# The first layer of a filter network: from VectorE, woven between weight splits, to a program of its own on GpSimd

## The chip, the cores and the metric

One core of a Trainium2 chip runs the whole program once. The metric is the device time of that run in microseconds (us). A kernel's time is the median of its runs. Engines are named as the profile names them: PE is the matrix engine (TensorE), DVE the vector engine (VectorE), ACT the scalar engine (ScalarE), POOL the GpSimd engine, SP the sync engine, which here only issues transfers. "SPq", "DVEq" and "ACTq" are those engines' sequencers.

## What is computed

The reference is two transformer-like blocks over 256 tokens of width 2048, all in float32. Almost all the time goes into products of token rows with large weight matrices. In the second block a convolution filter is made from positions by a small network, and its first layer is what the change moves:

```python
z = jnp.concatenate([t[:, None], jnp.cos(ang), -jnp.sin(ang)], axis=-1)   # 256 positions x 33
fr = freq.astype(f32)
h = jnp.sin(fr * (z @ w1 + b1))      # 33 -> 64: the first layer
h = jnp.sin(fr * (h @ w2 + b2))      # 64 -> 64
h = jnp.sin(fr * (h @ w3 + b3))      # 64 -> 64
h = h @ w4                           # 64 -> 2048 taps
```

`freq` and the inputs are scaled up so far (by 64) that the sum in front of the first sine must be more exact than float32. The kernel therefore adds the 33 products one by one with compensation: each product is split into parts whose rounding errors are kept, and each addition's error is worked out and added back.

## The kernel before, in words

**The stream of matrix products.** All large products run in one scheme (class Gemm, lines 83 to 107). A product is a row of groups of 512 output columns; with 2048 inputs a group is four chunks of 1 MB of weights. SP brings each chunk into one of four ring slots (`stream`, L357), issuing chunk k as soon as PE is done with chunk k-4. A chunk is used in two parts. For each part ACT makes the high half of the weights (`high`, L370, ring of four), DVE makes the low half by a subtraction (`low`, L379), and PE multiplies (`multiply_group`, L401): 12 matmuls a part of 128x512, 96 a group. ACT may write part p's high half only when PE is through with part p-4. So each engine works some parts ahead of PE, and the whole is one chain SP, ACT, DVE, PE.

**The stretch in question.** After the first block's input product comes `g_o` (4 groups, the first block's output weights), then, after a normalisation for which PE has to wait, `g_i2` (17 groups, numbered 0 to 16 here, the second block's input weights, 2048 to 8704 columns). Behind it comes the filter and the convolution.

**Work woven in.** DVE's side work is a generator, `filter_and_heads`, that `Spare` steps after each part's `low`, with a share of 1.4 us a part by costs that are written beside each `yield`. A generator may also yield a part number, before which it isn't stepped on. In the kernel before it clears `h3T` (the accumulator, 128 x 128: 64 hidden units of two halves of the positions), runs 11 steps `filter_sum(e)` of 3 inputs each, then `hidden_layer(0)` (bias, frequency and sine), then, at parts (12, 3) and (13, 3) of `g_i2`, `hidden_layer(1)` and `hidden_layer(2)`. For each input `filter_sum` issues 13 operations on 128x128 tiles (L1460, L1462, L1464) in 8 stages, with a semaphore wait at the end of each stage. Four of the 13 are the fused form, product and addition in one (L1464).

**Inputs of the sums.** `embedding(e)` (L2118 on, transfers at L2130) has SP bring the 3 inputs of step e, two transfers of 128 x 9 rows of values, into one of two slots of `z_k`. Step e of 2 and later waits first for `z_used` to be e-1, that is for step e-2 to be done with its slot. SP is one queue: while it waits there no weights are issued. The places in the stream are fixed by `EMBED_AFTER`: steps 0 and 1 behind the loads of group 0 of `g_o`, step 2 behind group 2, step 3 behind group 3, and steps 4 to 10 behind groups 1, 2, 3, 4, 6, 7 and 8 of `g_i2`. The last chunk of a group is issued when PE is done with the last chunk of the group before, so SP comes to a group's embedding just when PE starts that same group.

**The later layers.** PE computes the second and third layers as matmuls behind groups 11 and 12 of `g_i2` (L482 by way of `mm`), after waits for `sin1` and `sin2`, which DVE's sines signal.

Of the kernel before, what the change touches and what calls it, by code (L numbers as in the profile page):

```python
# [9 lines left out]
F32 = mybir.dt.float32  # L10
# [5 lines left out]
P = 128  # L16
# [25 lines left out]
EMB, HID = 33, 64  # L42
FK = 3
# [36 lines left out]
AT_AT = 124  # L80
MIX_AT = 146
LEAD = 3
LAYER_AFTER = (11, 12)
EMBED_AFTER = (0, 0, 2, 3, 5, 6, 7, 8, 10, 11, 12)
QK2_ROOT_GROUP = 15

# [51 lines left out]
def build(nc, a, out):  # L138
    Gemm.chunks = Gemm.groups_before = 0
    ctx = ExitStack()  # L140
    with ctx:
# [3 lines left out]
        def sb(name, shape, dt=F32, stack=ctx):  # L145
            return stack.enter_context(nc.sbuf_tensor(name, shape, dt))

        st = ExitStack()
# [3 lines left out]
        st = ExitStack()  # L152
# [25 lines left out]
        h3T = sb("h3T", [P, P])  # L178
        w1T = sb("w1T", [P, 3, 36])
# [3 lines left out]
        st = ExitStack()  # L183
# [3 lines left out]
        st = ExitStack()  # L187
# [2 lines left out]
        at_buf = sb("at_buf", [P, 4, P], F32, st)  # L190
        state = sb("state", [P, 2, 3, P], F32, st)
        dec = sb("dec", [P, NH, 4], F32, st)
        zero_t = sb("zero_t", [P, P], F32, st)
        st.close()
        st = ExitStack()
        sb("index_below", [P, HRING * HT * GW], F32, st)
# [6 lines left out]
        st = ExitStack()  # L203
# [3 lines left out]
        st = ExitStack()  # L207
        sb("filter_below", [P, HRING * HT * GW], F32, st)
        z_k = sb("z_k", [P, 2, 3, FK, P], F32, st)
        f_tmp = sb("f_tmp", [P, 6, P], F32, st)  # L210
        st.close()
        st = ExitStack()
        sc_s = sb("sc_s", [P, 4, SEQ], F32, st)
# [3 lines left out]
        st = ExitStack()  # L217
# [7 lines left out]
        st = ExitStack()  # L225
# [3 lines left out]
        st = ExitStack()  # L229
# [3 lines left out]
        st = ExitStack()  # L233
# [3 lines left out]
        st = ExitStack()  # L237
# [5 lines left out]
        st = ExitStack()  # L243
# [6 lines left out]
        st = ExitStack()  # L250
# [4 lines left out]
        st = ExitStack()  # L255
# [5 lines left out]
        st = ExitStack()  # L261
# [20 lines left out]
        st = ExitStack()  # L282
        hbuf = sb("hbuf", [P, TT, D], F32, st)
        st.close()
        st = ExitStack()
# [5 lines left out]
        st = ExitStack()  # L291
# [25 lines left out]
        g_i2 = Gemm([(w2v, 0)], KT, 17)  # L317
# [122 lines left out]
        def sig(name):  # L440
            if name not in signals:
                signals[name] = sem(name)
            return signals[name]

        block = ctx.enter_context(nc.Block())
# [34 lines left out]
        def _(pe):  # L480
# [117 lines left out]
            def recurrence():  # L598

                yield D_AT[0] - 1  # L600
                pe.wait_ge(sig("lf_ready"), TT)
                pe.wait_ge(sig("masks_in"), 48)
                b = bank(pe, "dec", "a")
                for h in range(NH):
                    for t in range(TT):
                        m = mm(b[:, 4 * h + 2 * t:4 * h + 2 * t + 2], lf[:, t, h * HD:h * HD + HD], ind[:])
                m.then_inc(filled, 1)
                for q, (n, t) in enumerate(((0, 0), (0, 1), (1, 0), (1, 1))):
                    if q == 3:
                        yield from turn_scaled(0)  # L610
                    for j in range(3):
                        yield D_AT[q] + j
                        mm(bank(pe, ("D", t, n, j), "a")[:, :], tri[:, j], lf[:, t, n * GW:n * GW + GW]).then_inc(filled, 1)
                yield from turn_scaled(1)
                pe.wait_ge(sig("zero_ready"), 1)
                for h in range(NH + 1):
                    if h < NH:
                        yield HEAD_AT + 2 * h
                        inside(h)
                    if h >= 1:  # L620
                        yield HEAD_AT + 2 * h + 1
                        recur(h - 1)
# [133 lines left out]

            for j in range(g_i2.groups):
                multiply_group(pe, g_i2, j, halves, turn_h2 if j == 0 else None)
                if j in LAYER_AFTER:
                    n = LAYER_AFTER.index(j)  # L760
                    pe.wait_ge(sig(f"sin{n + 1}"), 1)
                    mm(bank(pe, ("layer", n), "v")[:, 0:P], w23[:, n], h3T[:]).then_inc(filled, 1)

# [100 lines left out]
        def _(dve):  # L864
# [3 lines left out]
            def link(ins):  # L868

                links[0] += 1  # L870
                ins.then_inc(v_chain, 1)
                dve.wait_ge(v_chain, links[0])
# [215 lines left out]
            link(v.tensor_tensor(wl_, wh_, w_, ALU.subtract))  # L1088
            link(v.tensor_tensor(wh_, wh_, wl_, ALU.subtract))
            link(v.tensor_tensor(wl_, w_, wh_, ALU.subtract))  # L1090

            def before_products():

# [86 lines left out]
            def recurrence():  # L1180
# [9 lines left out]
                for t in range(TT):  # L1190
                    link(v.tensor_scalar(kc[:, t], kc[:, t], -1.0, 1.0, ALU.mult, ALU.add))
                link(v.memset(at_buf[:], 0.0))
                v.memset(zero_t[:], 0.0).then_inc(sig("zero_ready"), 1)
                for m, (n, t) in enumerate(((0, 0), (0, 1), (1, 0), (1, 1))):
                    yield D_AT[m] + 2 * LEAD
                    dve.wait_ge(sig("decays"), 4 * (m + 1))
# [241 lines left out]
                        v.tensor_tensor(x, pair[:], x, ALU.add).then_inc(evac[pair_of(gm, j)], 1)  # L1438
                return step

            def filter_sum(e):

                dve.wait_ge(sig("z_in"), 32 * (e + 1))
                p_, e_, s_, b_, d_, t_ = (f_tmp[:, q] for q in range(6))
                acc = h3T[:]
                for j in range(FK):
                    z_, zh, zl = (z_k[:, e % 2, q, j] for q in range(3))
                    w_, wh, wl = (w1T[:, q, e * FK + j:e * FK + j + 1] for q in range(3))
                    n = 13 * (FK * e + j)
                    for stage in (((p_, z_, w_, None),),  # L1450
                                  ((e_, zh, wh, p_), (s_, acc, p_, ALU.add)),
                                  ((e_, zl, wh, e_), (b_, s_, acc, ALU.subtract)),
                                  ((e_, zh, wl, e_), (d_, s_, b_, ALU.subtract), (t_, p_, b_, ALU.subtract)),
                                  ((e_, zl, wl, e_), (d_, acc, d_, ALU.subtract)),
                                  ((t_, t_, d_, ALU.add),),
                                  ((t_, t_, e_, ALU.add),),
                                  ((acc, s_, t_, ALU.add),)):
                        for o, x, y, last in stage:
                            if last is None:
                                i = v.tensor_scalar(o, x, y, None, ALU.mult)  # L1460
                            elif isinstance(last, ALU):
                                i = v.tensor_tensor(o, x, y, last)  # L1462
                            else:
                                i = v.scalar_tensor_tensor(o, x, y, last, ALU.mult, ALU.subtract if last is p_ else ALU.add)  # L1464
                            i.then_inc(sig("sum_step"), 1)
                            n += 1
                        dve.wait_ge(sig("sum_step"), n)
                        yield 0.33 * len(stage)
                dve.sem_inc(sig("z_used"), 1)

            def hidden_layer(n):

                if n:
# [13 lines left out]
            q2, k2 = heads(proj2, B_Q, NH), heads(proj2, B_K, 2)  # L1487

            def filter_and_heads():
                dve.wait_ge(sig("f_cols_in"), 16 * 8)  # L1490
                link(v.memset(h3T[:], 0.0))
                for e in range(EMB // FK):
                    yield from filter_sum(e)
                yield g_i2.part(1, 2)
                yield from hidden_layer(0)
                for n in range(1, 3):
                    yield g_i2.part(LAYER_AFTER[n - 1] + 1, 3)
                    yield from hidden_layer(n)
                yield g_i2.part(B_G // GW, 4)
                for j in range(B_Q // GW, B_G // GW):  # L1500
                    evacuated(dve, g_i2, j)
                yield from head_squares(q2, NH, HD, hs[:, :, 0:NH])
                yield from head_squares(k2, 2, HD, hs[:, :, NH:NH + 2])
                m = hs[:, :, 0:NH + 2]
                v.tensor_scalar(m, m, 1.0 / HD, EPS, ALU.mult, ALU.add).then_inc(sig("qk2_ms"), 1)
                yield g_i2.part(QK2_ROOT_GROUP, 4)
                dve.wait_ge(sig("ax_in"), 48)
                dve.wait_ge(sig("qk2_root"), 1)
                link(v.reciprocal(hs[:, :, 0:NH + 2], hs[:, :, 0:NH + 2]))
                yield from norm_and_rotate(q2, hs[:, :, 0:NH], gains2[:, 0], ax[:, 0], ax[:, 1], NH, HD, 2)  # L1510
                yield from norm_and_rotate(k2, hs[:, :, NH:NH + 2], gains2[:, 1], ax[:, 0], ax[:, 1], 2, HD, 2)
                dve.sem_inc(sig("qk2_roped"), 2)
# [591 lines left out]
        def _(sp):  # L2104
# [17 lines left out]
            def embedding(e):  # L2122

                if e == 0:
                    sp.wait_ge(sig("mix_a"), 2)
                if e >= 2:
                    sp.wait_ge(sig("z_used"), e - 1)
                for half in range(TT):
                    z = a["z"][half][:, FK * e:FK * e + FK]
                    sp.dma_start(z_k[half * HID:half * HID + HID, e % 2], z.partition_broadcast(HID)).then_inc(sig("z_in"), 16)  # L2130

            def beside_o(j):
                for e in range(EMB // FK):
# [19 lines left out]
            for j in range(g_d.groups):  # L2153
                o = slice(GW * j, GW * j + GW)
                evacuated(sp, g_d, j)
                sp.dma_start(out_rows[:, :, o], x_res[:, :, o]).then_inc(sig("out_written"), 16)
            sp.wait_ge(sig("out_written"), 16 * g_d.groups)


# [94 lines left out]
```

## Time and profile before

| What | us |
|---|---|
| median of 3 runs (2249.16 to 2251.08) | 2249.46 |
| the profiled execution's own time | 2251.36 |
| span of the profiled execution | 2249.6 |
| PE busy in it | 2091.2 (93%) |
| DVE busy | 1430.6 (64%) |
| ACT busy | 902.9 (40%) |
| POOL busy, 4 instructions | 0.2 |

The span is the time from the first to the last instruction in the trace. Times of rows are microseconds from its start; durations of single instructions are in ns where the row says min/median/max or mean ns. "idle before <-X" or "[.. <-X]" tells what ended the idle time of an engine in front of an instruction. A matmul row of PE overlaps the next one, so 96 matmuls of 389 ns take 21.8 us, not 37.

### The profile page before, as it was taken

How to read it: one execution, taken by the hardware profiler on the slowest of the kernel's cores; microseconds unless marked ns; L12 is line 12 of the kernel's file. 1: busy time of each engine (PE TensorE's matmuls, PEld its weight loads, DVE VectorE, ACT ScalarE, POOL GpSimd, SP SyncE). 2: the span in 40 equal slices, each digit the busy share in tenths (PEclk: the TensorE clock that was granted, in tenths of full speed). 3: DMA queues.
4: the chain of work that ended last, by engine and by line, in shares of the span. 5: the costliest groups of instructions: out<-in, count | busy, mean ns of one | idle time of the engine just before them, and what ended most of it. 6: DMA issues, size and time to landing. Idle time of an engine off the chain costs nothing.

```text
span 2249.6 us, 23590 instructions
## 1 busy us (share of the span) xinstructions
PE 2091.2 (93%) x9229; PEld 1644.1 (73%) x9229; DVE 1430.6 (64%) x2224; ACT 902.9 (40%) x1157; POOL 0.2 (0%) x4
## 2 busy tenths in 40 slices
PE   4889999999999798999977788989999999999999
PEld 0258787777878687887853567868888888878887
DVE  4857668677669787886877666555545454444443
ACT  2034523555644433444411343434444444443333
POOL 0000000000000000000000000000000000000000
PEclk8989979999999899999978999989999999999999
DMA  7867656544466475766630035545555555556554
GB/s 283 306 220 270 209 177 210 169 150 150 153 223 207 132 210 198 231 198 201 199 133 0 1 130 169 169 131 188 187 190 193 193 187 190 188 173 200 188 193 163
DMA packets 208498, 408.47 MB, mean 182 GB/s; under 512 B 10826, under 2 KB 16386, under 8 KB 207746
## 3 DMA queue, kind: packets, MB, share of 16 engines
q1 hardware_dynamic: 195056, 382.56, 51.7%
q10 hardware_dynamic: 13330, 24.40, 3.2%
q8 instruction: 73, 1.20, 0.2%
q14 instruction: 39, 0.31, 0.0%
HBM read 404.83 MB, written 2.10 MB: 181 GB/s over the span
## 4 chain that ended last, share of the span: by engine, by line
PE 82%; DVE 11%; DMA 3%; issue 1%; ACT 1%; ACTq 1%; SPq 0%; DVEq 0%
PE ps L401 74%; PE pm L482 5%; DVE raw_lo L379 3%; DMA raw<-in_w_in 2%; DVE mod_part L1144 1%; DMA raw<-in_ada_w 1%; PE ps L482 1%; PE pm L595 0%; DVE f_tmp L1462 0%; PE pm L494 0%; DMA proj<-in_hgrn_lb_logits 0%; PE pm L844 0%; DVE xtmp L1577 0%; ACT w_hi L370 0%; ACTq L1813 0%
## 5 line engine op out<-in xcount | busy, mean ns | idle before, releaser
L379 DVE TENSOR_TENSOR raw_lo<-raw,w_hi 128x1024 fp32r<-128x1024 f32 (+1 forms) x648 | 784.2, 1214 | 597.0 <-ACT w_hi L370 587.6
L370 ACT ACTIVATE w_hi<-raw 128x1024 fp32r<-128x1024 f32 (+1 forms) x648 | 678.2, 1050 | 892.1 <-PE ps L401 842.4
L401 PE MATMUL ps<-w_hi,h_hi 128*128 128x512 f32 (+1 forms) x2336 | 931.9, 399 | 42.1 <-DVE raw_lo L379 24.1
L401 PE MATMUL ps<-w_hi,h_lo 128*128 128x512 f32 (+1 forms) x2336 | 915.1, 392 | 0.0
L401 PE MATMUL ps<-raw_lo,h_hi 128*128 128x512 f32 (+1 forms) x2336 | 914.6, 392 | 0.0
L401 PEld LDWEIGHTS ps<-w_hi,h_hi 128*128 128x128 f32 x2336 | 444.9, 190 | 144.2 <-issue 31.8
L401 PEld LDWEIGHTS ps<-w_hi,h_lo 128*128 128x128 f32 x2336 | 444.8, 190 | 92.8
L401 PEld LDWEIGHTS ps<-raw_lo,h_hi 128*128 128x128 f32 x2336 | 445.3, 191 | 91.3 <-issue 3.8
L401 PE MATMUL ps<-w_hi,hid_hi 128*128 128x512 f32 x256 | 99.9, 390 | 1.8 <-DVE raw_lo L379 1.8
L401 PE MATMUL ps<-raw_lo,hid_hi 128*128 128x512 f32 x256 | 99.6, 389 | 0.0
L401 PE MATMUL ps<-w_hi,hid_lo 128*128 128x512 f32 x256 | 99.6, 389 | 0.0
L482 PE MATMUL ps<-raw,c_sig 128*1 128x512 f32 x128 | 67.2, 681 | 5.8 <-DMA raw<-in_ada_w 5.8
L401 PEld LDWEIGHTS ps<-w_hi,hid_hi 128*128 128x128 f32 x256 | 48.1, 188 | 12.0 <-DVE raw_lo L379 2.1
L401 PEld LDWEIGHTS ps<-w_hi,hid_lo 128*128 128x128 f32 x256 | 48.1, 188 | 10.1
L401 PEld LDWEIGHTS ps<-raw_lo,hid_hi 128*128 128x128 f32 x256 | 48.1, 188 | 9.7
L482 PEld LDWEIGHTS ps<-raw,c_sig 128*1 128x1 f32 x128 | 11.3, 92 | 59.2 <-issue 49.5
L1708 ACT ACTIVATE h_hi<-xtmp 128x256 fp32r<-128x256 f32 x88 | 32.8, 411 | 42.7 <-DVE xtmp L938 25.3
L1170 DVE SCALAR_TENSOR_TENSOR gate<-proj,c_sig,gate 128x512 f32<-128x512 f32 x64 | 48.0, 750 | 1.9
L1464 DVE SCALAR_TENSOR_TENSOR f_tmp<-z_k,w1T,f_tmp 128x128 f32<-128x128 f32 x132 | 46.1, 349 | 2.6
L1144 DVE SCALAR_TENSOR_TENSOR mod_part<-raw,c_sig,mod_part 128x512 f32<-128x512 f32 x56 | 42.1, 752 | 7.8 <-DMA raw<-in_ada_w 6.0
L1829 ACT ACTIVATE mod_row<-ps 1x512 f32<-1x512 f32 x8 | 4.7, 587 | 93.1 <-PE ps L482 93.1
L482 PE MATMUL ps<-mod_part,ones 128*1 128x512 f32 x16 | 9.0, 646 | 30.1 <-DVE mod_part L1144 30.1
(301 smaller groups left out, 1208.6 us busy)
## 6 DMA issues: line engine op xcount, KB each, us to landing
raw<-in_w_in SPq DMA_DIRECT2D x140, 1024.0 KB, 5.3
raw<-in_w_ffn_gate SPq DMA_DIRECT2D x44, 1024.0 KB, 5.2
raw<-in_w_ffn_up SPq DMA_DIRECT2D x44, 1024.0 KB, 5.2
raw<-in_w_ffn_down SPq DMA_DIRECT2D x44, 1024.0 KB, 5.1
raw<-in_ada_w SPq DMA_DIRECT2D x32, 1024.0 KB, 7.2
raw<-in_w_out SPq DMA_DIRECT2D x32, 1024.0 KB, 5.2
proj<-in_ada_w ACTq DMA_DIRECT2D x16, 1024.0 KB, 5.3
raw<-in_w_br_hyena SPq DMA_DIRECT2D x8, 1024.0 KB, 5.1
```

The lines of the kernel that those rows point to most:

```text
L370: nc.scalar.activation(w_hi[:, p % HRING, :, 0:gm.width(j)], raw[:, k % RING, e:e + HT, 0:gm.width(j)], ACT.Copy).then_inc(hi_done, 1)
L379: nc.vector.tensor_tensor(raw_lo[:, k % RING, e:e + HT, 0:gm.width(j)], raw[:, k % RING, e:e + HT, 0:gm.width(j)], w_hi[:, p % HRING, :, 0 ...
L401: mm = nc.tensor.matmul(ps[pair][:, t, 0:gm.width(j)], l[:, tok], r[:, i, 0:gm.width(j)], start=(k == 0 and q == 0), stop=(k == kt - 1 and ...
L482: return nc.tensor.matmul(o, l, r, start=start, stop=stop, **kw)
L1144: i = v.scalar_tensor_tensor(mod_part[:, g % 2], raw[:, c, k], w_, mod_part[:, g % 2], ALU.mult, ALU.add)
L1170: x = v.scalar_tensor_tensor(acc, gate_raw[i % 2][:, k], c_sig[:, CK * c + k:CK * c + k + 1], acc, ALU.mult, ALU.add)
L1464: i = v.scalar_tensor_tensor(o, x, y, last, ALU.mult, ALU.subtract if last is p_ else ALU.add)
L1708: s.activation(h_hi[:, k0 + k], xtmp[:, (k0 + k) % 4], ACT.Copy).then_inc(sig("x_hi"), 1)
L1829: s.activation(mod_row[0:1, g * GW:g * GW + GW], ps[g % 2][0:1, 0, :], ACT.Copy).then_inc(sig("mod_read"), 1)
```

## The change

DVE's `filter_sum` is taken out, and an equal sum is written as the program of POOL, which did nothing before. POOL has no fused product and addition here, so each of the four fused operations becomes two: 17 operations an input instead of 13, in 9 stages instead of 8. `f_tmp` gets a seventh tile for the extra product. POOL waits once for `w1_split`, clears `h3T`, and then runs the 11 steps without any pacing; each step waits for its own `z_in0` or `z_in1` and raises `z_used` at its end. On DVE the side work now begins at part (9, 0) of `g_i2`, where DVE waits for `z_used` to be 11 and goes on with `hidden_layer(0)`; the places of `hidden_layer(1)` and `(2)` and of PE's two matmuls are the same numbers as before, 12 and 13 with 3, and 11 and 12. An unused tile `zero_t`, its clearing on DVE and PE's wait for it are dropped.

```diff
-LAYER_AFTER = (11, 12)
+LAYER_AFTER = (9, 11, 12)
...
-        zero_t = sb("zero_t", [P, P], F32, st)
...
-        f_tmp = sb("f_tmp", [P, 6, P], F32, st)
+        f_tmp = sb("f_tmp", [P, 7, P], F32, st)
...
-                pe.wait_ge(sig("zero_ready"), 1)
...
-                if j in LAYER_AFTER:
-                    n = LAYER_AFTER.index(j)
+                if j in LAYER_AFTER[1:]:
+                    n = LAYER_AFTER.index(j) - 1
...
             link(v.tensor_tensor(wl_, w_, wh_, ALU.subtract))
+            dve.sem_inc(sig("w1_split"), 1)
...
-                v.memset(zero_t[:], 0.0).then_inc(sig("zero_ready"), 1)
...
             def filter_and_heads():
+                yield g_i2.part(LAYER_AFTER[0], 0)
                 dve.wait_ge(sig("f_cols_in"), 16 * 8)
-                link(v.memset(h3T[:], 0.0))
-                for e in range(EMB // FK):
-                    yield from filter_sum(e)
-                yield g_i2.part(1, 2)
+                dve.wait_ge(sig("z_used"), EMB // FK)
                 yield from hidden_layer(0)
                 for n in range(1, 3):
-                    yield g_i2.part(LAYER_AFTER[n - 1] + 1, 3)
+                    yield g_i2.part(LAYER_AFTER[n] + 1, 3)
                     yield from hidden_layer(n)
...
-                    sp.dma_start(z_k[half * HID:half * HID + HID, e % 2], z.partition_broadcast(HID)).then_inc(sig("z_in"), 16)
+                    sp.dma_start(z_k[half * HID:half * HID + HID, e % 2], z.partition_broadcast(HID)).then_inc(sig(f"z_in{e % 2}"), 16)
...
+        @block.gpsimd
+        def _(pool):
+            def filter_sum(e):
+
+                pool.wait_ge(sig(f"z_in{e % 2}"), 32 * (e // 2 + 1))
+                g = nc.gpsimd
+                p_, e_, s_, b_, d_, t_, q_ = (f_tmp[:, q] for q in range(7))
+                acc = h3T[:]
+                for j in range(FK):
+                    z_, zh, zl = (z_k[:, e % 2, q, j] for q in range(3))
+                    w_, wh, wl = (w1T[:, q, e * FK + j:e * FK + j + 1] for q in range(3))
+                    n = 17 * (FK * e + j)
+                    for stage in (((p_, z_, w_, ALU.mult), (e_, zh, wh, ALU.mult)),
+                                  ((e_, e_, p_, ALU.subtract), (s_, acc, p_, ALU.add), (q_, zl, wh, ALU.mult)),
+                                  ((e_, e_, q_, ALU.add), (b_, s_, acc, ALU.subtract)),
+                                  ((q_, zh, wl, ALU.mult), (d_, s_, b_, ALU.subtract), (t_, p_, b_, ALU.subtract)),
+                                  ((e_, e_, q_, ALU.add), (d_, acc, d_, ALU.subtract)),
+                                  ((q_, zl, wl, ALU.mult), (t_, t_, d_, ALU.add)),
+                                  ((e_, e_, q_, ALU.add),),
+                                  ((t_, t_, e_, ALU.add),),
+                                  ((acc, s_, t_, ALU.add),)):
+                        for o, x, y, op in stage:
+                            i = g.tensor_scalar(o, x, y, None, op) if op is ALU.mult else g.tensor_tensor(o, x, y, op)
+                            i.then_inc(sig("sum_step"), 1)
+                            n += 1
+                        pool.wait_ge(sig("sum_step"), n)
+                pool.sem_inc(sig("z_used"), 1)
+
+            pool.wait_ge(sig("w1_split"), 1)
+            nc.gpsimd.memset(h3T[:], 0.0).then_inc(sig("h3_clear"), 1)
+            pool.wait_ge(sig("h3_clear"), 1)
+            for e in range(EMB // FK):
+                filter_sum(e)
```

## Rows read from the trace of the kernel before

**Rows 1.** Busy time by stretch: length, PE, PEld, DVE, ACT, POOL, granted clock, DMA share, GB/s

```profile
757.00:846.00 89.00, 89.00 (x388) 73.46 (x389) 70.01 (x157) 36.20 (x43) 0.00 (x0) 0.97 0.62 187
846.00:890.00 44.00, 36.40 (x151) 29.34 (x151) 30.95 (x69) 17.26 (x17) 0.00 (x0) 0.92 0.59 197
890.00:1033.00 143.00, 143.00 (x634) 118.42 (x632) 116.73 (x252) 62.02 (x59) 0.00 (x0) 1.00 0.66 211
1057.00:1144.00 87.00, 87.00 (x386) 71.90 (x384) 69.08 (x138) 36.20 (x35) 0.00 (x0) 1.00 0.62 205
```

**Rows 2.** Chain that ended last, in time: start, length, what

```profile
772.71 16.39 PE ps L401 x72
...
866.04 0.61 SPq L2130
866.69 0.61 SPq L2130
867.35 8.63 DMA raw<-in_w_in
876.00 1.06 ACT w_hi L370
877.16 1.24 DVE raw_lo L379
878.53 154.45 PE ps L401 x672
1033.21 21.82 PE ps L401 x96
```

**Rows 3.** SP's waits from 640 to 1145: total, times, longest

```profile
SPq L2130 <- DVEq L1469: 38.7, 6, 16.7
```

**Rows 4.** SP's issues in time: start, length, what

```profile
649.06 2.78 SPq L2130 DMA_DIRECT2D z_k<-in_z  x4
...
787.59 1.26 SPq L2130 DMA_DIRECT2D z_k<-in_z  x2
...
837.43 1.26 SPq L2130 DMA_DIRECT2D z_k<-in_z  x2
...
946.64 1.26 SPq L2130 DMA_DIRECT2D z_k<-in_z  x2
```

**Rows 5.** PE's wait in front of group 5 of the second product (timeline)

```profile
878.53 0.76 PE L401 MATMUL ps<-w_hi,h_hi 128*128 128x512 f32 x1 [5.93 <-DVE raw_lo L379]
```

**Rows 6.** Busy time and clock around that wait (columns as in Rows 1)

```profile
878.50:881.00 2.50, 2.47 (x6) 2.02 (x7) 2.43 (x7) 2.29 (x3) 0.00 (x0) 0.50 1.05 389
881.00:884.00 3.00, 3.00 (x12) 2.36 (x11) 2.83 (x8) 1.18 (x2) 0.00 (x0) 0.75 0.57 212
```

**Rows 7.** The sum's tiles on DVE: ns min/median/max, first and last start

```profile
L1464 DVE SCALAR_TENSOR_TENSOR f_tmp<-z_k,w1T,f_tmp x132: 342/351/354, 670.8 to 994.2; 128x128 f32<-128x128 f32 x132
L1462 DVE TENSOR_TENSOR f_tmp<-f_tmp x132: 281/285/294, 673.3 to 996.2; 128x128 f32<-128x128 f32 x132
```

**Rows 8.** The inputs' transfers, issue to landing (view of z_k)

```profile
DMA to landing us min/median/max: 4.5/7.0/8.5
```

**Rows 9.** Small operations on POOL and ACT: busy us, mean ns or min/median/max

```profile
L2245 POOL MEMSET const-float32-1.0<- 128x1 f32 x1 | 0.1, 98 | 0.0
L1708 ACT ACTIVATE h_hi<-xtmp 128x256 fp32r<-128x256 f32 x88 | 32.8, 411 | 42.7 <-DVE xtmp L938 25.3
L1695 ACT ACTIVATE pm<-x_res x8: 582/602/603, 679.7 to 744.7; 128x512 f32<-128x512 f32 x8
```

**Rows 10.** DVE's weight splits from 656 to 964: busy, mean ns, idle before

```profile
L379 DVE TENSOR_TENSOR raw_lo<-raw,w_hi 128x1024 fp32r<-128x1024 f32 x104 | 126.8, 1225 | 40.5 <-ACT w_hi L370 37.7
```

**Rows 11.** DVE's splits for parts (9, 0) and (9, 1), timeline

```profile
960.80 1.23 DVE L379 TENSOR_TENSOR raw_lo<-raw,w_hi 128x1024 fp32r<-128x1024 f32 x1 [0.64 <-ACT w_hi L370]
...
963.46 1.23 DVE L379 TENSOR_TENSOR raw_lo<-raw,w_hi 128x1024 fp32r<-128x1024 f32 x1 [0.26 <-ACT w_hi L370]
```

**Rows 12.** PE's wait for the second sine, behind group 12 (timeline)

```profile
1056.66 0.49 PE L482 MATMUL pm<-h3T,w 128*128 128x128 f32 x2 [1.65 <-DVE h3T L916]
```

More of the change, by code:

```diff
@@ L1439, in residual @@
                 return step
[L1441 to L1469, printed above, removed]
             def hidden_layer(n):
```

## The prediction

> **What bounds the kernel now.** I read the page first (PE busy 93% of the span), then busy time by stretch, then the chain, then SP's waits. In stretches of the second input product PE is busy all the time: 143.00 of 143.00 us and 87.00 of 87.00 [rows 1]. A group of 96 matmuls takes 21.82 us [rows 2]. There DVE, at 116.73 of 143 us, costs nothing. The one stretch with a loss beside the change is 846 to 890, where PE is busy for 36.40 of 44 us [rows 1]. The chain says why: SP issued the inputs of step 7 at 866.04, the weights behind them landed 8.63 us after 867.35, then came ACT, DVE, and PE at 878.53 [rows 2], after 5.93 us idle [rows 5]. SP had been held by DVE's `z_used`: 38.7 us in 6 waits, the longest 16.7 [rows 3]. So the sum's pace on DVE, not DVE's own load, costs PE time, by way of SP's queue.
>
> **How much there is to gain.** Group 0 of `g_i2` ends 48 matmuls behind 772.71, at 772.71 + 48 x 0.2275 = 783.6. Without a loss group 5 would start at 783.6 + 4 x 21.82 = 870.9; it starts at 878.5, and its first six matmuls take 2.5 us, 0.42 us each against 0.2275, at a granted clock of 0.50, the 1.2 GHz level that it fell to in the idle time [rows 6]. Seven groups take 154.45 us against 152.7 [rows 2], so 1.7 us go there. The whole loss is 7.6 + 1.7 = 9.3 us. That is all that a fast enough POOL can give back: 0.4% of the time.
>
> **Part by part, what costs nothing.** The 13 operations an input leave DVE (429 in all, at 285 to 351 ns [rows 7], some 131 us). By themselves they give nothing, since PE hides them. The sines move in one respect: `hidden_layer(0)` is pinned to part (9, 0), but PE's matmuls stay behind groups 11 and 12. `hidden_layer(1)` still starts at (12, 3), so the 1.65 us that PE waits for the second sine [rows 12] stay. The clearing of `zero_t` and PE's wait for it, the one extra semaphore increment of DVE, POOL's clearing of `h3T` during the first block: nothing. All of these lie beside the matmuls of the first block; without that cover each is one small operation, under 1 us together. The seventh tile of `f_tmp` costs room, not time. SP issues the same 22 transfers at the same places; they now wait on POOL.
>
> **The added wait.** At (9, 0) DVE waits for the eleventh step. Behind it in DVE's queue stands the split for (9, 1), and PE waits for that. In the trace DVE starts that split at 963.46 [rows 11], while PE starts (9, 1) at 1033.21 - 3 x 21.82 + 2.73 = 970.5. A split takes 1.23 us, so DVE has to be free by 969.2 in the time of this trace, and by 969.2 - 9.3 = 959.9 in a flow without the loss. If the last step ends at time S, the change is S - 969.2, and never less than -9.3.
>
> **When can the last step end?** Its inputs are issued when PE starts group 8: 783.6 + 7 x 21.82 = 936.3 without the loss (946.64 in the trace [rows 4], late by the loss). They take 7.0 us [rows 8], so they are there at 943.3 plus the issue, 944. Only if POOL does three inputs in 16 us does DVE not wait at all. The first inputs are issued at 649.06 [rows 4] and are there at 656, when POOL can start; DVE before started its first at 670.8 [rows 7].
>
> **The price of an operation on POOL** is in no row: POOL has four clears of one element a partition, 98 ns each [rows 9]. Bounds: not below what DVE takes for the same tile, 285 ns, in a chain about 0.30 us; at the dear end what ACT takes for four times as much, 602 ns. Between them lies ACT's 411 ns for 128x256 [rows 9], another engine with a fixed cost of its own on a small tile. I take this, 0.41 us, waits included: 17 x 0.41 = 7.0 us an input, 21 a step, 231 in all. The ends are 5.1 and 10.2 us an input. By the Trainium skill (GPSIMD Engine Reference, "Elementwise — side-by-side cycle accounting") an addition of two tiles costs some 2.6 cycles an element at 1.2 GHz, which I estimate at 0.28 us for 128 elements before dispatch; no run here shows it yet, and it would not move the sum.
>
> **POOL beside DVE** is in no row either, and is the largest term. Both read two tiles of the same memory. From 656 to part (9, 0) DVE runs 103 splits of 1.225 us [rows 10], 126 us. The ends are: none of it holds POOL up, or all of it does. No row is near to either; I choose the dear end, as my own judgement, for the forecast and keep the other as a rival. Then the last step ends at 656 + 231 + 126 = 1013. On the way SP is held too: a step takes 21 us and the splits of one group beside it 8 x 1.225 = 9.8, so 31 us a step against a group's 21.8, and from about step 6 on PE starves behind SP each time. That is the same delay and not another one: POOL has its inputs a step ahead and is never idle in it, so only the end of its work counts. The change is 1013 - 969.2 = 43.8 us, and 1.7 us, the price above, for the lower clock behind the long stall: +45.5. The profiled execution took 2251.4 us (span 2249.6 and 1.8 around it), so it would take 2296.9; it stood 1.9 us above the median, so the forecast for the median is 2295.
>
> The Trainium skill (SBUF — State Buffer, "Who interferes with whom") has a rule for this: DVE and GpSimd share a pair of memory ports under an exclusive lock, and a DVE operation with two inputs in SBUF and a GpSimd operation that reads SBUF block each other fully, for the whole instruction. It speaks against this change, and would make of it what the dear end makes, 2295; without the rule the same prices give 2248 (below). Nothing in this trace can show it, as POOL reads nothing there.
>
> **The rivals.**
> 1. No holding up, 7.0 us an input. The last three steps follow step 8's inputs (issued at the start of group 6, 892.7, there at 900): 900 + 63 = 963, and the last can't end before 944 + 21 = 965. The change is 965 - 969.2 = -4, and 1.7 us for the clock behind a stall of 5: about 2247, or 2248 where the issues come a little late. For it: DVE has idle gaps, 40.5 us in front of those splits [rows 10]. Against: two hard-working readers of one memory.
> 2. POOL is as quick as DVE and undisturbed: 15.3 us a step, last step at 959.3, DVE free in time, gain 9.3: 2240. For it: the trace has the loss and the change removes its cause. Against: it needs both the cheapest price and no disturbance. This is the side faster than before; it decides for itself below 16 us a step.
> 3. POOL is slow, 10.2 us an input. Undisturbed: 656 + 337 = 993, +24 and the clock: 2275. Disturbed: 993 + 126 = 1119, +150 and the clock: 2401. For it: two operations where DVE had one, on an engine with no history here. Against: the 98 ns of its small clears [rows 9].
> 4. The change does not do what it says: the sine two groups sooner brings nothing, since the matmul behind it has not moved. That is in every case above.
>
> What speaks against the forecast most is that POOL's waits between stages (9 an input) may lie under DVE's splits, so that less than 126 us are lost. At 60% the last three steps, which can't begin before 900, take 3 x (21 + 0.6 x 9.8) = 81 us: S = 981, +12 and the clock, 2263. At 8 us an input and all of it lost, S = 656 + 264 + 126 = 1046: 2328. The likeliest case's own range is 2263 to 2330.
>
> **How the numbers follow.** Forecast (POOL late because DVE and POOL shut each other out, in whole or in large part): 0.46. Rival 1: 0.12. Rival 2: 0.20. Rival 3: 0.22, of which undisturbed 0.12 and disturbed 0.10. A measurement of this kernel can tell about 0.2%, 4.5 us, from no change. Faster by more: rival 2, 0.20. Within: rival 1, 0.12. Slower: the rest, 0.68. The range goes from 2239 (rival 2, whose 9.3 us are a floor, and rounding) to 2340, above the forecast's own upper end; it leaves out the disturbed rival 3 and a little of the rest.
>
> **What would show it.** In the profile after, I look at POOL's operations: start to start 0.41 us inside a stage when DVE is idle, and gaps or long operations while a split runs. DVE's splits should be 1.23 us or begin late. SP's waits at L2130 for POOL should grow well above 38.7 us in total; DVE should stand at part (9, 0) for tens of us, and PE's granted clock should fall there. The stretch of `g_i2` should end near 1144 + 45. If POOL does a step in under 16 us, the forecast is wrong and 2240 right; if DVE's wait is a few us and SP's waits are nearly gone, rival 1 is; if POOL's operations take 0.6 us with DVE idle, rival 3.

## The result: 2343.27 us, and the profile after

The changed kernel takes 2343.27 us (median of 4 runs, 2341.69 to 2343.78) against 2250.27 for the kernel before on the same chip: a ratio of 1.0407, 95% interval 1.0388 to 1.0426, so 93.0 us slower. The direction was forecast; the forecast value, 2295, and the upper end of the range, 2340, were both too low.

The waits of SP and PE between 640 and 1240 us of the kernel after (who waited for whom: total, times, longest):

```profile
SPq L2096 <- POOLq L2151: 144.9, 8, 29.1
```

```profile
PE ps L400 <- DVE raw_lo L378: 89.3, 9, 39.5
PE pm L493 <- DVEq L986: 8.9, 1, 8.9
PE ps L400 <- DVE h_lo L921: 7.8, 1, 7.8
```

SP's waits at the embeddings have grown from 38.7 us [rows 3] to 144.9, and now stand against POOL. PE waits 89.3 us for splits of weights, the longest time 39.5, where the longest before was 5.93 [rows 5].

Busy time by stretch, kernel after (columns as in rows 1):

```profile
757.00:846.00 89.00, 78.79 (x334) 64.54 (x335) 48.06 (x60) 36.98 (x47) 83.64 (x115) 0.91 0.58 182
846.00:890.00 44.00, 32.78 (x137) 26.68 (x136) 14.25 (x11) 11.28 (x11) 41.02 (x64) 0.88 0.33 109
890.00:1019.00 129.00, 98.95 (x413) 80.60 (x412) 43.86 (x33) 39.52 (x39) 119.85 (x184) 0.90 0.55 174
1019.00:1062.00 43.00, 4.38 (x12) 3.07 (x10) 1.67 (x6) 3.57 (x4) 37.36 (x78) 0.54 0.08 30
```

The figure in front of the granted clock is POOL's: it is busy with only short gaps through all four, while PE falls to 98.95 of 129 us and then to 4.38 of 43. In [rows 1] PE was at 143.00 of 143.00. DVE has the time that the change freed, and nothing to do with it. The granted clock in the last stretch is 0.54, near the 1.2 GHz level.

The end of the sum and what DVE does then, kernel after (timeline: start, length, engine, line, what, idle before):

```profile
1059.55 0.45 POOL L2147 TENSOR_TENSOR h3T<-f_tmp 128x128 f32<-128x128 f32 x1
```

```profile
1016.97 1.23 DVE L378 TENSOR_TENSOR raw_lo<-raw,w_hi 128x1024 fp32r<-128x1024 f32 x1 [17.40 <-ACT w_hi L369]
1060.16 0.29 DVE L1446 TENSOR_SCALAR h3T<-h3T,f_cols 128x128 f32<-128x128 f32 x1 [41.97 <-POOLq L2151]
...
1061.59 1.23 DVE L378 TENSOR_TENSOR raw_lo<-raw,w_hi 128x1024 fp32r<-128x1024 f32 x1
```

```profile
1062.87 0.80 PE L400 MATMUL ps<-w_hi,h_hi 128*128 128x512 f32 x1 [39.49 <-DVE raw_lo L378]
```

The split at 1016.97 is that of part (9, 0). Then DVE stands for 41.97 us at the added wait, until POOL's last operation ends at 1060.0. PE's part (9, 1) starts at 1062.87. In the kernel before it started at 970.5 (worked out in the prediction from [rows 2]), so PE is 92.4 us behind when the sum is done. The profiled executions as a whole differ by the same 92.4 us (spans of 2342.0 and 2249.6), the medians by 93.0.

POOL's operations in that last stretch, where no other engine has work, and then one place where DVE works too (timeline of the kernel after):

```profile
1043.49 0.45 POOL L2147 TENSOR_TENSOR f_tmp<-f_tmp 128x128 f32<-128x128 f32 x1
1043.90 0.45 POOL L2147 TENSOR_TENSOR f_tmp<-h3T,f_tmp 128x128 f32<-128x128 f32 x1
1044.33 0.60 POOL L2147 TENSOR_SCALAR f_tmp<-z_k,w1T 128x128 f32<-128x128 f32 x1
1045.02 0.45 POOL L2147 TENSOR_TENSOR f_tmp<-f_tmp 128x128 f32<-128x128 f32 x1
...
1050.61 0.45 POOL L2147 TENSOR_TENSOR h3T<-f_tmp 128x128 f32<-128x128 f32 x1
1051.16 1.18 POOL L2147 TENSOR_SCALAR f_tmp<-z_k,w1T 128x128 f32<-128x128 f32 x2
```

```profile
870.65 0.46 POOL L2147 TENSOR_TENSOR f_tmp<-f_tmp 128x128 f32<-128x128 f32 x1
870.73 4.00 DVE L378 TENSOR_TENSOR raw_lo<-raw,w_hi 128x1024 fp32r<-128x1024 f32 x3 [18.00 <-ACT w_hi L369]
871.07 1.44 POOL L2147 TENSOR_TENSOR f_tmp<-f_tmp,h3T 128x128 f32<-128x128 f32 x1
...
872.60 2.51 POOL L2147 TENSOR_SCALAR f_tmp<-z_k,w1T 128x128 f32<-128x128 f32 x1
```

Alone, an addition takes 0.45 us (0.40 to 0.43 from start to start inside a stage, 0.55 across a wait) and a product 0.60 (0.57 from start to start). An input takes 1051.16 - 1042.22 = 8.94 us. Beside DVE's splits the same addition takes 1.44 and the same product 2.51. A reader should look at single rows and the median, not at the mean: the page gives the products a mean of 792 ns, while none of the 165 lies between 750 and 850 ns; the median is 602.

From the first operation at 657.4 to 1060.0 POOL needs 402.6 us. 33 inputs at 8.94 are 295.0, and each change to a new step adds about 0.1, so some 296 in all; the other 107 are what the company of DVE costs. Not all of it is the splits: DVE's other operations with two inputs run in the same time, and the next section parts the two. A split on DVE grew too, to a mean of 1312 ns from the 1225 of [rows 10] (view of lines, DVE, 656 to 1061):

```profile
L378 DVE TENSOR_TENSOR raw_lo<-raw,w_hi 128x1024 fp32r<-128x1024 f32 x103 | 133.8, 1312 | 183.7 <-ACT w_hi L369 183.3
```

### The profile page after: what moved, and what is told of

Its sections match the earlier page's. It is cut to its first block, busy times and chain, and to the rows that moved or that the text cites. A ratio compares the mean times of both kernels' runs of the same rounds, so it can differ in the third digit from the quotient of the medians.

```text
span 2342.0 us, 23626 instructions
## 1 busy us (share of the span) xinstructions
PE 2099.8 (90%) x9229; PEld 1649.9 (70%) x9229; DVE 1332.1 (57%) x1793; ACT 902.1 (39%) x1157; POOL 376.1 (16%) x566
## 4 chain that ended last, share of the span: by engine, by line
PE 70%; POOL 16%; DVE 8%; issue 2%; DMA 2%; ACTq 1%; ACT 1%; SPq 0%; DVEq 0%; POOLq 0%
PE ps L400 63%; POOL f_tmp L2147 15%; PE pm L481 5%; DVE mod_part L1143 1%; DVE raw_lo L378 1%; POOL h3T L2147 1%; DMA raw<-in_ada_w 1%; PE ps L481 1%; PE pm L594 0%; DMA proj<-in_hgrn_lb_logits 0%; PE pm L842 0%; ACTq L1779 0%; DVE xtmp L1543 0%; PE pm L493 0%; DMA z_k<-in_z 0%
## 5 line engine op out<-in xcount | busy, mean ns | idle before, releaser
L378 DVE TENSOR_TENSOR raw_lo<-raw,w_hi 128x1024 fp32r<-128x1024 f32 (+1 forms) x648 | 792.3, 1228 | 752.6 <-ACT w_hi L369 745.7
L2147 POOL TENSOR_SCALAR f_tmp<-z_k,w1T 128x128 f32<-128x128 f32 x165 | 129.9, 792 | 655.3 <-DMA z_k<-in_z 644.3
L2147 POOL TENSOR_TENSOR f_tmp<-f_tmp 128x128 f32<-128x128 f32 x264 | 161.0, 615 | 13.3
L2147 POOL TENSOR_TENSOR f_tmp<-h3T,f_tmp 128x128 f32<-128x128 f32 x66 | 41.6, 630 | 0.0
```

The source lines that it names most:

```text
L378: nc.vector.tensor_tensor(raw_lo[:, k % RING, e:e + HT, 0:gm.width(j)], raw[:, k % RING, e:e + HT, 0:gm.width(j)], w_hi[:, p % HRING, :, 0 ...
L2147: i = g.tensor_scalar(o, x, y, None, op) if op is ALU.mult else g.tensor_tensor(o, x, y, op)
```

## The experiments

**One-input splits.** Does DVE hold POOL up by its two inputs, or is POOL slowed by any company?

```diff
-            nc.vector.tensor_tensor(raw_lo[:, k % RING, e:e + HT, 0:gm.width(j)], raw[:, k % RING, e:e + HT, 0:gm.width(j)], w_hi[:, p % HRING, :, 0:gm.width(j)].bitcast(F32), ALU.subtract)\
...
+            lo, x = raw_lo[:, k % RING, e:e + HT, 0:gm.width(j)], raw[:, k % RING, e:e + HT, 0:gm.width(j)]
+            if gm is g_o or (gm is g_i2 and j <= 9):
...
+                    i = nc.vector.tensor_reduce(lo, x.unsqueeze(3), AX.X, ALU.add)
+            else:
+                i = nc.vector.tensor_tensor(lo, x, w_hi[:, p % HRING, :, 0:gm.width(j)].bitcast(F32), ALU.subtract)
+            i.then_inc(lo_done, 1)
```

> The kernel after, but while POOL sums (second output product and groups 0 to 9 of the second input product) DVE's split is a reduction over one element that reads one tensor instead of a subtraction of two: the low half of the weights is then a copy of the weights, so products are not the reference's. Theory (a DVE operation with two inputs in SBUF and a POOL operation that reads shut each other out): POOL's operations stay at 0.45 and 0.60 us throughout, an input takes 9.0 us, the last step ends near 980 (three steps of 27 us from the landing of step 8's inputs at 900), time near 2262. Rival (POOL is slowed by any DVE work, or by PE, ACT and the transfers): POOL's work still takes some 400 us, time near 2343.

Measured: 2269.48 us, ratio 1.0089 (1.0076 to 1.0102). The splits, and POOL's commonest additions and its products, in this run (view of lines, DVE from 656 to 1061; then POOL over the whole run):

```profile
L381 DVE TENSOR_REDUCE raw_lo<-raw 128x1024 fp32r<-128x1024 f32 x108 | 131.1, 1219 | 129.8 <-ACT w_hi L369 128.9
```

```profile
L2152 POOL TENSOR_TENSOR f_tmp<-f_tmp 128x128 f32<-128x128 f32 x264 | 123.0, 471 | 13.3
L2152 POOL TENSOR_SCALAR f_tmp<-z_k,w1T 128x128 f32<-128x128 f32 x165 | 103.7, 633 | 672.9 <-DMA z_k<-in_z 662.1 <-POOL h3T L2152 2.1
```

The reductions are as long as the subtractions were (1219 against 1225 ns), PE, ACT and the transfers do the same work, and yet POOL's additions are at a mean of 471 ns instead of 615 and the products at 633 instead of 792. The rival falls: POOL loses most of its time to the form of DVE's split, and not to company as such. That it is the second input that counts, this run alone can't say; the next one shows that the number of inputs is not all.

POOL's waits for its inputs in this run:

```profile
POOL f_tmp L2152 <- DMA z_k<-in_z: 662.1, 2, 641.4
```

Its first operation starts at 654.6 and its last ends at 983.1, which is 328.5 us, of which it stood for 20.7 us (the second of the two waits, from 771.8 on) before the inputs of step 4 came. So its work took 307.8 us, 12 more than the 296 it needs alone. Against the 402.6 of the kernel after, the two-input form of the splits costs POOL 95 us, 0.92 for each of 103; the 12 are left for all the rest, DVE's other two-input operations among it.

The last step was expected to end at 980, and the time is 7 us above the expectation. The later end makes 3 us of that, and DVE's five small operations of the first sine before the next split (1060.16 to 1061.59 above) 1.4. The other 3 are not explained; the profiled execution, at 2267.86 us, lies 1.6 under the median.

**One input, in a shorter form.** The kernel after once more, with the same place changed to another one-input form, which takes DVE less time. The edit differs from that of the run above in one line:

```diff
...
+                i = nc.vector.tensor_scalar(lo, x, 1.0, None, ALU.mult)
...
```

> The kernel after with the split, while POOL sums, replaced by a product of one SBUF tensor with 1.0 (the low half is then a copy of the weights): one input, and a form that DVE may run at twice the rate, 0.6 us or so. Theory (a one-input DVE operation holds POOL up only if it runs at twice the rate; it then does for its whole length): about 0.5 us for each of 103, the last step ends near 1005, time near 2286. Rival (only two inputs matter): 2262.

Measured: 2293.15 us, ratio 1.0185 (1.0166 to 1.0204). DVE's splits from 656 to 1061 (count, busy, mean), and POOL's last kind of operation (ns min/median/max, first and last start) in this run:

```profile
L380 DVE TENSOR_SCALAR raw_lo<-raw 128x1024 fp32r<-128x1024 f32 x109 | 83.5, 770 | 187.9 <-ACT w_hi L369 187.5
```

```profile
L2151 POOL TENSOR_TENSOR h3T<-f_tmp x33: 454/463/871, 668.1 to 1008.3; 128x128 f32<-128x128 f32 x33
```

These are shorter than the reductions, 770 against 1219 ns, with the same one input, and they cost POOL far more. Its first operation starts at 656.9 and its last ends near 1009: 352 us, without a wait for inputs between. That is 56 above the 296 alone, and 44 above the 307.8 of the run with reductions, so about 0.43 us for each of the 103 splits in front of the wait. The rival, that only two inputs matter, falls. The theory is borne out in part: these splits do hold POOL up, but by less than their own 0.77 us. The time is 24 us above that with the longer reductions.

**A later wait.**

```diff
-                yield g_i2.part(LAYER_AFTER[0], 0)
+                yield g_i2.part(10, 4)
```

> The kernel after with DVE's wait for the sums at part (10, 4) instead of (9, 0). Theory (the change costs what the last step is later than the place where DVE waits): 12 more parts of PE work, 33 us, lie in front of the wait; their splits make POOL's end 12 us later, near 1072, so PE's wait shrinks from 39.5 to about 17 and the time to about 2320. Rival (the loss was already made at SP, in front of part (9, 0)): the time stays near 2343.

Measured: 2324.72 us, ratio 1.0332 (1.0318 to 1.0346). PE's waits for splits in this run (total, times, longest):

```profile
PE ps L400 <- DVE raw_lo L378: 68.8, 9, 18.3
```

The longest fell from 39.5 to 18.3 us. The last step ended near 1067 instead of 1060, as the splits in the added parts slowed POOL, so of the 33 us of cover some 26 should be won. The profiled executions show 25.0: PE starts group 12 at 1102.96 instead of 1127.93. The medians differ by only 18.6. Most of the gap between the two is that this run's profiled execution (2321.69) lies 3.0 us under its median, and that eight matmuls far behind took 6.24 us in it against 3.71 (see below on such a difference). The place of the wait is a dial on the loss. It can't be expected to bring the loss to nothing, as PE's matmul for the second layer stands behind group 11; no run went so far.

**A third of the inputs.** Only 11 of 33 are summed; the transfers stay.

```diff
-                for j in range(FK):
+                for j in range(1):
...
-                    n = 17 * (FK * e + j)
+                    n = 17 * e
```

> The kernel after with only the first of each step's three inputs summed (11 of 33), transfers unchanged. Theory: a step takes 12 us with its share of DVE's splits, no wait at part (9, 0) and none at SP, so the time falls to the floor, 9.3 us under the kernel before: near 2240. Rival (POOL beside DVE also delays DVE and through it PE, or the new wait costs by itself): 2249 or more.

Measured: 2241.3 us, ratio 0.9967 (0.9954 to 0.9979), so 8.2 us faster than the kernel before. POOL disturbed and was disturbed as before (its products had a mean of 915 ns, and DVE's splits one of 1260), but it was almost in time: DVE waited for it once, for 4.2 us, where no wait was expected, and PE hardly at all. So neither the added wait nor the slower splits cost anything that this run can show. DVE's and PE's waits in it (total, times, longest):

```profile
DVE h3T L1446 <- POOLq L2151: 4.2, 1, 4.2
```

```profile
PE ps L400 <- DVE raw_lo L378: 3.7, 3, 1.8
```

**Three slots for POOL's inputs.** `z_k` gets a third slot, SP waits for step e-3; three of the scratch tiles move into the tile of masks.

```diff
-        z_k = sb("z_k", [P, 2, 3, FK, P], F32, st)
+        z_k = sb("z_k", [P, 3, 3, FK, P], F32, st)
...
-                if e >= 2:
-                    sp.wait_ge(sig("z_used"), e - 1)
+                if e >= 3:
+                    sp.wait_ge(sig("z_used"), e - 2)
```

> The kernel after with three slots for the inputs. Theory (SP's 144.9 us of waits for POOL and DVE's wait at part (9, 0) are one delay, that of POOL's last step): SP's waits go, DVE's single wait grows from 42 to some 100 us, the last step still ends near 1060 and the time stays near 2343, within 5 us. Rival (SP's stalls add a loss of their own): 2320 or less.

Measured: 2342.94 us, ratio 1.0412 (1.0394 to 1.043). SP's waits for POOL and DVE's wait at part (9, 0) in this run:

```profile
SPq L2096 <- POOLq L2151: 59.4, 3, 28.0
```

```profile
DVE h3T L1446 <- POOLq L2151: 68.9, 1, 68.9
```

SP waits 85.5 us less than with two slots and DVE 27 us more. Here the expectation missed: it had SP's waits gone and DVE's at some 100 us, and 59.4 and 68.9 were measured. But the last step ended at 1058.4, and the time is the same to 0.3 us. So the stalls at SP were not a second loss: they only shared out the one delay that POOL's end sets.

**Three slots, sum on DVE.** The kernel before with the same third slot; the arithmetic is unchanged.

```diff
...
-            p_, e_, s_, b_, d_, t_ = (f_tmp[:, q] for q in range(6))
+            p_, e_, s_, b_, d_, t_ = [f_tmp[:, q] for q in range(3)] + [tri[:, q] for q in range(3)]
...
-                if e >= 2:
-                    sp.wait_ge(sig("z_used"), e - 1)
+                if e >= 3:
+                    sp.wait_ge(sig("z_used"), e - 2)
```

> The kernel before (sum on DVE) with three slots for the inputs instead of two (three scratch tiles lie in the tile of masks, which nobody reads any more), so that SP waits for step e-3. Theory (the 9.3 us lost in the kernel before came from SP's waits): SP's waits nearly go, time near 2240. Rival (the loss is from DVE's load of splits and sums together): 2249.

Measured: 2239.67 us, ratio 0.9951 (0.9935 to 0.9967). SP's waits for the sum, and the stretches that answer to [rows 1]:

```profile
SPq L2130 <- DVEq L1469: 0.3, 1, 0.3
```

```profile
846.00:890.00 44.00, 44.00 (x196) 36.44 (x195) 37.13 (x84) 18.80 (x18) 0.00 (x0) 1.00 0.68 208
890.00:1033.00 143.00, 143.00 (x634) 118.41 (x633) 115.74 (x248) 63.30 (x61) 0.00 (x0) 1.00 0.67 212
```

PE is busy for all 44.00 us where it had 36.40, at the full clock, with DVE at 37.13 of 44 us. The loss of the kernel before was SP's queue held by a slot that was not free, and not DVE's load. This version is faster than both kernels, by 9.9 us against the one before, about 0.5%.

## Why the prediction was right in its direction and wrong in its size

**Right: what there was to gain, 9.3 us.** The two runs that remove SP's waits without bringing long new ones are 8.2 and 9.9 us faster. In their profiled executions `g_i2`, from its first matmul to its last, takes 377.4 and 377.3 us, against 387.5 in the kernel before.

**Right: that the place of the wait turns POOL's last step into PE's time.** The rule was S - 969.2 and 1.7 us for the clock. With the measured S of 1060.0 it gives 92.5; the measured change is 93.0. That they agree so closely is in part luck. The rule leaves out five operations of the sine (1060.16 to 1061.59) that go ahead of the split that PE waits for, 1.4 us, and at the end of `g_i2` the profiled execution is 94.7 us behind (1238.98 against 1144.26). Behind that it gets 2.3 us back, nearly all of it in eight matmuls of the convolution (chain that ended last; before, then after):

```profile
1222.71 5.94 PE pm L482 x8
```

```profile
1317.20 3.71 PE pm L481 x8
```

The granted clock over them is 0.62 before and 1.00 after. The change has no part in this: of the other six profiled executions four show 3.71 us there and two some 6.2. That SP's stalls are the same delay was right too, by the run with three slots.

**Right: that DVE and POOL shut each other out.** The prediction took the dear end by judgement, with no row for it, 126 us for 103 splits of 1.225. Measured are 107 us for all of DVE's company, of which the splits make 95, 0.92 us each, three quarters of what was put down for them; the other 12 belong to operations that the prediction left out. Whether the missing quarter lies under POOL's waits between stages, as it said, no run shows. DVE lost too: its subtractions grew from a mean of 1225 to 1312 ns, while the reductions stayed at 1219. The Trainium skill (SBUF — State Buffer, "Who interferes with whom") states that a DVE operation with two SBUF inputs, or one in a two-port mode, and a GpSimd operation that reads SBUF block each other fully, and that a `tensor_reduce` on trn2 never does so. The three forms of the split agree with it: 95 us lost to the splits with two inputs, 44 to the product with a constant, and with the reduction additions at a mean of 471 ns against 450 or so alone, at least part of which belongs to the two-input operations that stayed. That the product ran in a two-port mode no view shows; its 770 ns against the reduction's 1219 fit one.

**Wrong: the price of an operation on POOL.** This is the step that failed. The prediction took 0.41 us an operation with waits included, from ACT's 411 ns for 128x256 [rows 9], and so 7.0 us an input and 231 in all. Measured are 8.94 an input, 0.53 us an operation, and 296 in all: 65 us more. The company cost 19 us less than it was given, and the start came 1.4 us later (657.4 for 656); this leaves 47 us of error in S, 1060 for 1013, which is nearly the whole error of the forecast, 48. So the second error hid a part of the first. The bounds of the price, 5.1 to 10.2 us an input, did hold it; the range of the time did not, because its upper end, 2340, lay only 12 us above what 8 us an input gives (2328), and the case above it, price and disturbance both dear (2401), was left out with a chance of 0.10. Two dear ends of independent terms had been treated as a tail, though 0.53 us lies only 0.12 above the value taken.

What could have been read more sharply in [rows 9]: ACT's 411 ns is the length of one operation, with no wait on its result behind it, and it was taken with waits included. Nine waits an input on POOL's own results cost about 0.14 us each (0.55 us from start to start where there is a wait, 0.41 where not), some 1.3 us of the 1.9 that were missing. The rest is that the products take 0.60. The 98 ns of the small clears, set against a dear price in rival 3, were no guide either: POOL cleared the 128x128 tile of `h3T` in 204 ns, and adds two such tiles in 450.

**The rivals.** Rivals 1 and 2 needed POOL undisturbed, and it was not. The run with reductions comes near to making that condition of rival 1 true, and takes 2269 us instead of the 2248 that the cheaper price gave. At 8.94 us an input a step takes 26.9 us against PE's 21.8 for a group, so even then the sum comes late. Rival 3, disturbed, came nearest in kind: the price was dear and the company too, though each less than in its 2401. Of its sign, operations of 0.6 us with DVE idle, the products show 0.60 and the additions 0.45. That every fused operation has to become two on POOL was taken as given; no run tried another way.

## What to carry to other kernels

Work that an engine does in the shade of another costs nothing, and moving it to an idle engine gives back nothing but the waits that hang on it: look for who waits for its result, here SP's queue, and free that (one more slot: 0.5%) before moving any work. Before an engine is given a long chain beside another, work out three things: its price with a wait behind each stage, what it shares with the engine that will be busy at the same time, and the time at which its last result falls due; then take both dear ends together as a case of its own. Where a fixed place waits for a free-running engine, its lateness is paid once, but not always at that place: here PE's wait behind it was 39.5 us, and the rest of the 93 had been paid before it, behind SP's full slots.

## What the runs showed of the hardware that was not expected

- On POOL a product of a 128x128 tile with a value per partition takes longer than an addition of two such tiles: 0.60 us against 0.45, alone.
- A DVE operation's length tells little of what it costs POOL: a one-input reduction of 1219 ns leaves the additions at a mean of 471 ns; a one-input product with a constant, of 770 ns, takes about 0.43 us more than that from POOL each time, and a two-input subtraction of 1312 ns about 0.92 more.
- A blocked operation shows as a longer one in POOL's rows (0.45 becomes 1.44, 0.60 becomes 2.51), not as idle time in front of it. POOL's "busy" share is therefore no measure of its work: 376 us are shown as busy in 402.6, while 33 inputs alone need 296 with the gaps between their operations, which add up to 27.
